# A decoder block on one core: late expert rows gathered from the first step of the value stage on, at steps set by how many buffers they have, and the first weights split ahead of the first values

## The reference

```python
def peer_ffn(xn, wq, sub_keys, u_tab, v_tab):
    q = (xn @ wq).reshape(B, S, PEER_HEADS, 2, PEER_HALF)
    s = jnp.einsum('bshpd,hpnd->bshpn', q, sub_keys).astype(jnp.float32)
    top_v, top_i = lax.top_k(s, PEER_TOPK)
    ...
    experts = i1 * PEER_NKEYS + i2
    gates = jax.nn.softmax(cand_v, axis=-1).astype(xn.dtype)
    ...
        act = jax.nn.gelu(jnp.einsum('td,tkd->tk', xb, u_tab[eb]))
        return jnp.einsum('tk,tkd->td', gb * act, v_tab[eb])
```

## Time and profile before

| what | value |
|---|---|
| median of 3 runs | 2824.9 us (2822.78 to 2829.67) |
| the profiled execution, its own time | 2819.92 us |
| its span in the trace | 2818.2 us |
| PE busy | 2302.0 us (82%) |
| DVE busy | 2091.9 us (74%) |
| ACT busy | 1235.5 us (44%) |
| POOL busy | 703.0 us (25%) |
| value stage (PE, L1611 and L1638) | 2080.36 to 2806.34 us |

### The profile page before, as it was taken

How to read it: one execution, slowest core, us unless ns; L and a number is a source line. 1 busy time by engine, 2 the same in 40 slices (tenths; PEclk the granted TensorE clock), 3 DMA queues, 4 the chain that set the end, 5 groups by cost and what they waited for, 6 DMA issues and landing times.

```text
span 2818.2 us, 39707 instructions
## 1 busy us (share of the span) xinstructions
PE 2302.0 (82%) x14809; PEld 2089.1 (74%) x14809; DVE 2091.9 (74%) x2718; ACT 1235.5 (44%) x1871; POOL 703.0 (25%) x394
## 2 busy tenths in 40 slices
PE   7999999999999999999999000013389999999998
PEld 6989999999999888899799000013268877877776
DVE  6786456665645755754469999999966899999995
ACT  3554544444544443443454000159854434444443
POOL 0000000000000100010004786878841234434330
PEclk9999999999999999999999555555599999999999
DMA  7444565555565555554459997999837999999994
GB/s 209 150 140 131 174 184 166 157 155 150 162 197 164 177 189 189 182 182 142 135 194 346 391 398 306 393 406 389 336 135 262 374 398 416 422 422 422 421 418 169
DMA packets 325176, 729.37 MB, mean 259 GB/s; under 512 B 23256, under 2 KB 265136, under 8 KB 267072
## 3 DMA queue, kind: packets, MB, share of 16 engines
q1 hardware_dynamic: 277648, 386.18, 41.1%
q0 software_dynamic: 46912, 340.81, 30.2%
q10 hardware_dynamic: 496, 0.84, 0.1%
HBM read 725.66 MB, written 2.10 MB: 258 GB/s over the span
## 4 chain that ended last, share of the span: by engine, by line
PE 60%; DVE 23%; DMA 9%; issue 4%; ACT 1%; POOL 1%; SPq 1%; DVEq 0%; ACTq 0%; POOLq 0%
PE bank L400 32%; DVE b_u_ring L2054 13%; PE bank L1611 12%; PE bank L423 8%; DMA b_late_row<-in_peer_v,b_idx_all 5%; DMA b_late_row<-in_peer_u,b_idx_all 4%; PE bank L424 4%; DVE b_w_both L382 1%; DVE b_v_lo L2106 1%; PE bank L1396 1%; DVE b_late_sum L2131 1%; SPq L657 1%; DVE b_late_row L2122 1%; PE bank L1482 1%; DVE b_rstd L461 1%
## 5 line engine op out<-in xcount | busy, mean ns | idle before, releaser
L382 DVE TENSOR_TENSOR b_w_both<-b_raw,b_w_both 128x1024 fp32r<-128x1024 f32 x464 | 569.4, 1245 | 466.0 <-ACT b_w_both L377 464.9
L377 ACT ACTIVATE b_w_both<-b_raw 128x1024 fp32r<-128x1024 f32 x464 | 484.7, 1057 | 586.4 <-PE bank L400 391.9
L400 PE MATMUL bank<-b_act_both,b_w_both 128*128 128x256 f32 x4224 | 518.3, 285 | 6.8 <-DVE b_w_both L382 6.8
L400 PEld LDWEIGHTS bank<-b_act_both,b_w_both 128*128 128x128 f32 x4224 | 512.2, 193 | 9.7 <-DVE b_w_both L382 4.8
L1179 ACT ACTIVATE b_v_hi<-b_v_raw 128x1024 fp32r<-128x1024 f32 x256 | 271.9, 1062 | 418.8 <-PE bank L1611 337.6
L749 POOL DMA_INDIRECT b_u_ring<-in_peer_u,b_idx_all x192 | 416.7, 2170 | 152.9 <-DVE b_dots L2054 76.2
L2054 DVE CUSTOM_DVE_ANT_0 b_u_ring<-b_u_ring,b_xnN 128x2048 f32<-128x2048 f32 x192 | 436.8, 2280 | 0.0
L400 PE MATMUL bank<-b_att_both,b_w_both 128*128 128x256 f32 x3072 | 375.2, 284 | 0.0
L400 PEld LDWEIGHTS bank<-b_att_both,b_w_both 128*128 128x128 f32 x3072 | 371.8, 193 | 0.6 <-issue 0.3
L2106 DVE TENSOR_TENSOR b_v_lo<-b_v_raw,b_v_hi 128x1024 fp32r<-128x1024 f32 x256 | 307.8, 1220 | 72.9 <-ACT b_v_hi L1179 72.9
L1611 PE MATMUL bank<-b_v_hi,b_e_hi 128*128 128x512 f32 x1024 | 317.8, 392 | 1.7 <-DVE b_e_lo L2111 1.7
(11 more groups left out here) (326 smaller groups left out, 2736.7 us busy)
## 6 DMA issues: line engine op xcount, KB each, us to landing
b_v_raw<-in_peer_v SPq DMA_DIRECT2D x128, 1024.0 KB
b_raw<-in_w_in SPq DMA_DIRECT2D x208, 512.0 KB, 4.3
b_raw<-in_w_proj_dsa SPq DMA_DIRECT2D x32, 512.0 KB, 3.5
b_raw<-in_w_proj_gla SPq DMA_DIRECT2D x32, 512.0 KB, 3.5
b_raw<-in_w_xk SPq DMA_DIRECT2D x32, 512.0 KB, 4.6
b_raw<-in_w_out SPq DMA_DIRECT2D x32, 512.0 KB, 4.3
b_raw<-in_w_xv SPq DMA_DIRECT2D x32, 512.0 KB, 4.4
b_raw<-in_w_xq SPq DMA_DIRECT2D x32, 512.0 KB, 4.6
```

What stands on the lines that cost most here:

```text
L377: act.activation(w_hi[:, q], raw[:, UQ * c + q], ACT.Copy).then_inc(w_high, 1)
L382: dve.tensor_tensor(w_lo[:, q], raw[:, UQ * c + q], w_hi[:, q].bitcast(F32), ALU.subtract).then_inc(w_split, 1)
L400: mm = pe.matmul(proj[c][:, n], lhs, rhs, start=(q == 0 and n == 0 and k == 0 and t == 0), stop=(q == UQ - 1 and k == UK - 1 and t == 2), ...
```

## The change

- Gathering begins when the tables that place late row 0 overwrites are no longer read (all `oct_rows` and `oct_cols` made, all gates exponentiated), that is, just ahead of step 0, in a new place (over masks and tables of constants, which is why small tiles move and the constant `eps` is copied once).
- There is one buffer at first, a second from row 7 (`e_split` 8, step 27), and a third and a fourth from rows 18 and 19 (both `e_split` 16, step 59).
- Rows 0 to 6 are worked off at steps 1, 6, 11, ... 31, rows 7 to 17 at steps 33, 36, 38, 41, ... 58, and rows 18 to 127 from step 60 on, spread over 186 steps (the last at step 244).
- The weights of batch 0 are split ahead of the values of step 0.

```diff
-LATE_STEP = 30
+LATE_ALONE = (1, 6, 11, 16, 21, 26, 31)
+LATE_PAIRED = (33, 36, 38, 41, 43, 46, 48, 51, 53, 56, 58)
 TILES_GROW = {48: 24}
-ROWS_GROW = {17: 16, 36: 24}
+ROWS_GROW = {len(LATE_ALONE): 8, 18: 16, 19: 16}
...
-    late_row = [sb(f"late_row{n}", [D], at) for n, at in enumerate((RAW, RAW + 64 * K, RAW + 72 * K, RAW + 16 * K))]
-    late_sum = sb("late_sum", [D], RAW + 8 * K)
+    late_row = [sb(f"late_row{n}", [D], at) for n, at in enumerate((SML + 4 * C_MASK, RAW, RAW + 72 * K, RAW + 8 * K))]
+    late_sum = sb("late_sum", [D], RAW + 64 * K)
...
-    row_place, row_back = places(LATE_ROWS, 2, ROWS_GROW)
+    row_place, row_back = places(LATE_ROWS, 1, ROWS_GROW)
...
-        first = LATE_STEP + 2 * PTOP
-        span = STEPS - 2 * PER_BATCH - first - 6
+        ahead = LATE_ALONE + LATE_PAIRED
+        first, rest = ahead[-1] + 2, LATE_ROWS - len(ahead)
+        span = STEPS - 2 * PER_BATCH - 2 - first
         if n < first:
-            return [m for m in range(PTOP) if LATE_STEP + 2 * m == n]
-        return [m for m in range(PTOP, LATE_ROWS) if first + span * (m - PTOP) // (LATE_ROWS - PTOP) == n]
+            return [ahead.index(n)] if n in ahead else []
+        return [m for m in range(len(ahead), LATE_ROWS) if first + span * (m - len(ahead)) // rest == n]
...
-        pool.wait_ge(sem("e_split"), 8)
+        pool.wait_ge(sem("rows_by_vector"), OCTETS)
+        pool.wait_ge(sem("cols_by_pool"), OCTETS - COLS_BY_VECTOR)
+        pool.wait_ge(sem("gate_exped"), GROUPS)
...
-            elif m >= 2:
+            elif m >= 1:
                 pool.wait_ge(sem("late_used"), m - row_back[m] + 1)
...
+        act.wait_ge(sem("consts_landed"), 16)
+        act.activation(eps, const(EPSC), ACT.Copy)
...
+        weights_high(0)
         for n in range(STEPS):
             value_high(n)
-            if n == 1:
-                weights_high(0)
...
             if m == PTOP:
-                dve.wait_ge(sem("e_split"), 16)
+                dve.wait_ge(sem("e_split"), 8)
...
+        weights_low(0)
         for n in range(STEPS):
             if n % PER_BATCH == 3 and n // PER_BATCH + 1 < NKEYS // BATCH:
                 weights_low(n // PER_BATCH + 1)
             value_low(n)
-            if n == 1:
-                weights_low(0)
```

More of the change, by code:

```diff
@@ L316, in hybrid_block @@
     chosen = sb("chosen", [2, PTOP, PTOP], R + 2 * K)
-    idx_all = sb("idx_all", [GROUPS * PTOP], s1 + K + 384, U32)
-    gates_all = sb("gates_all", [GROUPS * PTOP], s1 + 2 * K + 384)
+    idx_all = sb("idx_all", [GROUPS * PTOP], s1 + 9 * K, U32)
+    gates_all = sb("gates_all", [GROUPS * PTOP], s1 + 7 * K + 384)
     s0 = s1 + 3 * K + 384
@@ L334, in hybrid_block @@
     isel_late = sb("isel_late", [2, PTOP], s2 + 480)
-    dots = sb("dots", [EARLY * PTOP], s1)
+    dots = sb("dots", [EARLY * PTOP], s1 + 10 * K + 64)
     gate_sums = sb("gate_sums", [GROUPS], s2 + 160)
     gate_parts = sb("gate_parts", [GROUPS], s2 + 224)
-    assert base + s2 + 608 <= nc.sbuf_usable_end
+    eps = sb("eps", [1], s1 + 10 * K)
+    assert s2 + 608 <= s1 + 9 * K and base + s1 + 11 * K <= nc.sbuf_usable_end
+    assert SML + 4 * C_MASK + 4 * D <= s1 + 4 * K + 384
     ident = consts[:, C_IDENT:C_IDENT + P]
@@ L1255, in _ @@
         act.wait_ge(sem("out_summed"), 1)
-        act.activation(stat[:, 6:8], stat[:, 6:8], ACT.Sqrt, scale=1.0 / D, bias=const(EPSC)).then_inc(sem("out_root"), 1)
+        act.activation(stat[:, 6:8], stat[:, 6:8], ACT.Sqrt, scale=1.0 / D, bias=eps).then_inc(sem("out_root"), 1)
     @block.tensor
```

## The result

| | before | change |
|---|---|---|
| median | 2824.87 us (2818.3 to 2829.67, 5 runs) | 2806.09 us (2804.46 to 2813.66, 5 runs) |
| the profiled execution, its own time | 2819.92 us | 2804.46 us |
| its span | 2818.2 us | 2802.7 us |

The ratio is 0.9942, 95% interval 0.9922 to 0.9962: faster by some 16 us (0.0058 of 2825; the two medians lie 18.8 us apart, the two profiled executions 15.5). The prediction was 2810 us.

What follows compares the result with a forecast made beforehand. The value stage was taken to lose 26.2 us, mainly to late rows (14.2) and full DMA (9.8). Gains of 1.2 (opening), 5.2 (late rows less new-buffer cost) and 8.3 (long stretch) sum to 14.7: 2810 us, range 2801 to 2819.

Steps and rivals of the forecast that it cites:

- Opening, gain 1.2: Start of the value stage: splitting the first weights early removes a 1.73 us PE wait, row 0 costs 0.5; gain 1.2 us.
- Rows 1 to 17, no wait: Steps 6 to 58: a 5-step buffer cycle leaves 11.1 us to land, landings need 9.7 at most; no wait.
- New buffers, cost 9.0: Step 59: PE waits 4.6 us for row 18, 1.9 for row 19, plus 2.5 of lower clock; cost 9.0 us.
- Long stretch, 1.5 of 9.8 left: From 2360 to 2740 us: demand falls to 420.8 GB/s, so 1.5 of 9.8 us lost remain; gain 8.3 us.
- The rival that the stretch stays as it was: Long stretch: the queues' rate bounds it whatever the schedule, 9.8 us stay lost; gain 6.4, 2818.5 us; chance 0.10.
- the doubled wait: Rival at step 59: row 18 lands only after 14.5 us, 7.3 us more lost; gain 7.4, 2817.5 us; chance 0.08.
- the too short cycle: Rival for rows 0 to 17: landings of 14.5 us overrun the 5-step cycle; 19 us slower, 2844 us; chance 0.04.
- Held-up gathers: Rival at rows 0 and 18: gather issues wait for DVE, up to 2.3 us each; gain 10.1, 2814.8 us; chance 0.05.
- End: End of the value stage: the last row moves from step 240 to 244, and this stays hidden from PE.
- Sum: Whole kernel: gains of 1.2, 5.2 and 8.3 make 14.7 us; 2805.2 for the profiled execution, 2810 against the median.
- rows too late: Kernel before, 2220 to 2360 us: DVE waits for late rows and PE stands still; 14.2 us lost, all to go.
- DMA full: Kernel before, 2360 to 2740 us: the schedule asks 432.6 GB/s, the queues move 421; 9.8 us lost.

Runs made afterwards that it cites:

- experiment 1: The change, but with the first weights split behind the values of step 1 again, as before; median 2805.3 us, ratio to before 0.9952.
- Experiment 8: The change, but with single-buffer rows every 3 steps instead of 5 and the second buffer from row 10; median 2818.7 us, ratio to before 0.9984.
- experiment 3: The change, but with rows 18 to 127 spread over 178 steps instead of 186; median 2821.5 us, ratio to before 1.0001.
- experiment 6: The schedule of experiment 3, but each late gather brings half a row, which DVE reads twice; one run, 2802.6 us.
- experiment 7: The schedule of experiment 3 with whole gathers, but DVE uses only half of each late row; one run, 2819.6 us.
- experiment 4: The kernel before with its old schedule, but the fourth buffer comes at step 59 instead of 91; median 2820.7 us, ratio to before 0.9994.
- experiment 2: The change, but the third and fourth buffers are first used by rows 20 and 21, not 18 and 19; median 2803.0 us, ratio to before 0.9942.

## Why the prediction was right

- *Opening, gain 1.2.* Right in kind, a little too low: 1.8 (experiment 1). Row 0 cost 0.2 us and not 0.5. It landed in 7.8 us, just under the 8.3 to 9.7 that I used; POOL issued it 0.77 behind its tables, not 0.3. DVE waited 2.23 us for it, where I had said under 2.
- *Rows 1 to 17, no wait.* Right. With one gather in flight landings took 5.8 to 8.5 us, with two up to 10.2, all under the 11.1 of a 5-step cycle. Experiment 8 shows the price if they are not.
- *New buffers, cost 9.0.* The mechanism was right, the size too high: 6.9. The first wait was as worked out (landing 8.9 for 9, PE 4.41 for 4.6). The second, 1.9 us for row 19, did not come: I had taken it to land 5.0 us behind row 18, from an event with full queues; it landed 2242.67 + 9.4 = 2252.1, 2.5 us behind row 18, when DVE had ended that and was at the next `v_lo`, so it was there 0.9 us before DVE came to it at 2253.02. So the sign "PE waits for `v_lo` twice" was wrong. The lower clock cost what I took for it: 6.9 less the wait of 4.41 is 2.5.
- *Long stretch, 1.5 of 9.8 left.* Right: 1.9. That the cause is the transfers and not DVE is shown by experiments 3, 6 and 7, that it is the bytes asked per step by the change beside experiment 3. The rival that the stretch stays as it was falls, and so do the doubled wait and the too short cycle.
- *Held-up gathers.* Row 18 was issued 0.95 us behind the start of `e_lo`, as in the earlier trace rows, and its issue took 1.68 us. It landed in 8.9 us all the same. No 2.3 us are to be seen; the rule of the Trainium skill, "SBUF — State Buffer", section "Who interferes with whom", costs at most the 0.7 us here that I had from the trace. The same section of the Trainium skill infers that making descriptors needs the write side of the shared ports, of which a `tensor_tensor` takes only the read side; DVE ran `e_lo` and a `v_lo` beside this issue, both `tensor_tensor`, and the trace agrees but for those 0.7 us. In the full queues behind it some issues took 3.4 us and one 5.62 (at 2310.64), longer than any single instruction of DVE there (2.35); what holds those was not tested.
- *End.* Hidden, as worked out: the last multiple ended at 2755.9, 9.8 us ahead of PE (8.8 foreseen).
- *Sum.* 14.7 us on the profiled execution; it is 15.5 (2819.92 less 2804.46). The stage and its opening gave 17.5 (from the start of the seeding to the end, 731.4 before and 713.9 after), and the 2.1 us by which the part ahead of it was later took some back. So it is in part luck that the profiled execution came within 1 us of the sum: the stage gained 2.8 us more than I had said, 2.1 of them at the new buffers and 0.6 in the opening, and the late start hid most of it.
- *What I split wrongly* is the 14.2 us of "rows too late" and the 9.8 us of "DMA full". By its trace, experiment 4 removes the first cause, and half of that time is lost again further on. The sum held since the change slows the pace and adds the buffers together.

## What to carry to other kernels

Where two streams share full queues, write the demand of the schedule in bytes per step and set it against the rate that the trace shows; here 432.6 against 421 GB/s explained the loss, and 3% less demand, by starting early with one buffer, took most of it away. A transfer into room that is freed late must not be wanted before one whole landing (9 us here, more than three steps) has passed: two rows more in the old buffers were 4.8 us cheaper, in the traces, than two new buffers used at once. And where an engine is 95% busy beside a full queue, halve the one and then the other before saying which bounds.

## What the hardware did that I had not expected

- A gather of 1 MB, alone on its queue beside the stream of tiles, landed in 5.6 to 6.8 us mostly, but in 7.8 and 8.5 (change) and 7.9 and 9.3 (experiment 8) now and then. A cycle has to be laid out for the late ones.
- The granted clock fell to 1.2 GHz behind PE's waits of 2.08 and 2.87 us (before), 4.41 (change), 3.0 (experiment 6) and 3.47 and 3.42 (experiment 8). It stayed at 2.4 GHz behind the wait of 1.73 us that opens the stage in before and experiment 1, and from 2080 to 2780 us in experiment 2, whose longest wait was 1.6 us.
- The part ahead of the value stage, unchanged, ended at 2080.2 to 2091.9 us in the traces of the kernels that have the same instructions there, and most of the difference was there at 1500 us. What sets this is open.
